# Operand starts in SBUF moved by 64 bytes: activations and split weights of a kernel's last block

## The reference, cut to what matters

```python
# 256 tokens, d = 1024, float32; two layers and then one more block
def first_block(x, ...):
    for layer in range(2):
        h = h + 0.5 * swiglu(rms_norm(h, g), w_gate, w_up, w_down)      # d_ff = 2816
        ...                                                # a convolution or attention, memory attention, w_o
        h = h + 0.5 * swiglu(rms_norm(h, g), w_gate, w_up, w_down)
def second_block(x, ...):                                  # "the last block"
    p = rms_norm(x, norm_pre) @ w_in                       # q, k, v of two mixers, gates
    ya = norm(diff_attention(...)) * silu(...)
    yb = norm(sigmoid(...) * mlstm(...)) * silu(...)
    merged = sigmoid(ga) * (ya @ w_a) + sigmoid(gb) * (yb @ w_b)
    return x + rms_norm(merged @ w_out, norm_post)
```

## The kernel before

| operand | place | modulo 256 |
| --- | --- | --- |
| whi, wlo, every slot | 0 | 128 |
| xh, xl (view of x0 and x1) | 64 | 192 |
| rh, rl | 0 | 128 |
| g in feed-forward 1, 2, 4 | 64 | 192 |
| g in feed-forward 3 | 0 | 0 |

## Time and profile before

### The profile page before, as it was taken

The page is one execution under the profiler, slowest core; times in us unless marked ns, Lnnn a source line. Parts: engine busy times, 40 slices in busy tenths (PEclk is TensorE's granted clock), DMA queues, the critical chain, the costliest instruction groups (busy, mean ns, idle before and its releaser), DMA issues.

```text
span 1186.7 us, 18987 instructions
## 1 busy us (share of the span) xinstructions
PE 1179.2 (99%) x7592; PEld 1043.9 (88%) x7592; DVE 862.0 (73%) x1213; ACT 677.7 (57%) x1036; POOL 65.5 (6%) x86
## 2 busy tenths in 40 slices
PE   9999999999999999999999999999999999999998
PEld 8888889969988888888888888998888899879996
DVE  7977766886887767787766677677776668666875
ACT  6766644547665555655554457566554545566463
POOL 1501000200010000000000022000000000000000
PEclk9999999999999999999999999999999999999999
DMA  8865656664656656656655553256655665536450
GB/s 305 305 195 180 194 176 204 210 174 137 202 189 187 190 173 195 202 172 212 192 173 173 190 177 125 74 194 193 192 184 178 194 215 173 185 125 184 144 171 35
DMA packets 65398, 215.85 MB, mean 182 GB/s; under 512 B 8352, under 2 KB 12064, under 8 KB 65184
## 3 DMA queue, kind: packets, MB, share of 16 engines
q1 hardware_dynamic: 62608, 210.64, 55.5%
q10 hardware_dynamic: 2704, 4.02, 1.0%
HBM read 212.70 MB, written 1.93 MB: 181 GB/s over the span
## 4 chain that ended last, share of the span: by engine, by line
PE 97%; DVE 1%; DMA 1%; ACT 0%; issue 0%; SPq 0%; POOL 0%; DVEq 0%; POOLq 0%
PE psum L509 96%; DMA raw<-in_slots 1%; PE psum L920 0%; DVE small L2308 0%; PE psum L1062 0%; ACT whi L1253 0%; PE psum L880 0%; PE psum L970 0%; PE psum L1011 0%; PE psum L1203 0%; PE psum L673 0%; DVE qkc L2678 0%; DVE wlo L1864 0%; PE psum L956 0%; ACT vn L1637 0%
## 5 line engine op out<-in xcount | busy, mean ns | idle before, releaser
L509 PE MATMUL psum<-x,whi 128*128 128x512 f32 (+1 forms) x2512 | 633.2, 343 | 0.2 <-DVE x L1935 0.2
L1864 DVE TENSOR_TENSOR wlo<-raw,whi 128x1024 fp32r<-128x1024 f32 (+2 forms) x402 | 474.2, 1191 | 162.1 <-ACT whi L1253 159.1
L1253 ACT CAST whi<-raw 128x1024 fp32r<-128x1024 f32 (+2 forms) x402 | 405.4, 1022 | 156.0 <-PE psum L509 151.2
L509 PE MATMUL psum<-x,wlo 128*128 128x256 f32 x1960 | 430.7, 279 | 0.0
L509 PEld LDWEIGHTS psum<-x,wlo 128*128 128x128 f32 x1960 | 366.7, 188 | 58.2 <-DVE wlo L1980 0.4
L509 PEld LDWEIGHTS psum<-x,whi 128*128 128x128 f32 x2512 | 382.1, 188 | 2.3 <-issue 1.2
L509 PE MATMUL psum<-g,whi 128*128 128x512 f32 x704 | 218.7, 392 | 0.0
L509 PEld LDWEIGHTS psum<-g,wlo 128*128 128x128 f32 x704 | 132.2, 188 | 29.5
L509 PE MATMUL psum<-whi,x 128*128 128x512 f32 (+1 forms) x512 | 140.6, 375 | 0.0
L509 PE MATMUL psum<-g,wlo 128*128 128x256 f32 x704 | 139.2, 279 | 0.0
L509 PEld LDWEIGHTS psum<-g,whi 128*128 128x128 f32 x704 | 106.8, 188 | 0.0
(11 more groups left out here) (317 smaller groups left out, 775.6 us busy)
## 6 DMA issues: line engine op xcount, KB each, us to landing
raw<-in_slots SPq DMA_DIRECT2D x371, 512.0 KB, 4.2
raw<-in_slots SPq DMA_DIRECT2D x16, 384.0 KB, 3.3
raw<-in_slots SPq DMA_DIRECT2D x16, 256.0 KB, 2.9
h<-conv_mem SPq DMA_DIRECT2D x8, 284.0 KB, 5.0
mkv<-in_mem ACTq DMA_DIRECT2D x1, 1024.0 KB, 12.4
memt<-in_mem_cols ACTq DMA_DIRECT2D x1, 1024.0 KB, 15.7
conv_mem<-hc SPq DMA_DIRECT2D x3, 288.0 KB, 2.2
h<-conv_mem SPq DMA_DIRECT2D x4, 142.0 KB, 2.9
```

Source lines behind the costliest of these rows:

```text
L509: return pe.matmul(o, l, r, start=start, stop=stop, skip_group_check=True)
L1253: act.copy(held(B.whi[:, i % SPLIT, :], *n), held(B.raw[:, i % RAW, :], *n)).then_inc(*s.hi.now(i))
L1864: dve.tensor_tensor(held(B.wlo[:, i % SPLIT, :], *n), held(B.raw[:, i % RAW, :], *n), held(B.whi[:, i % SPLIT, :], *n).bitcast(F32), ALU.s ...
```

## The change

The last block's normed activations (generation "w2") are written to and read from `rh[0]`/`rl[0]`, place 0, instead of `xh[0]`/`xl[0]`, place 64. In TensorE's code this is index 2 of a list that now has `rh[0]` behind `xh`. The split weights of 33 narrow slots (QK2, GATE2, AQK2, GAB2) stand 16 elements (64 bytes) further on in their buffers; those of the row form (VB2, VA2, ZO2) stay at the start. Each of the five buffers of `whi` and `wlo` is 32 elements (128 bytes) longer for that. To make room, `ln1` and `diag`, constants and scratch of the first layer's convolution, move into that layer's own space, and `ctap` into half of an attention buffer of the last block.

```diff
+PLACE = 32
+MOVED = {QK2 + i for i in range(9)} | {AQK2 + i for i in range(8)} | {GAB2 + i for i in range(16)}
...
+def place(i):
+    return 16 if i in MOVED else 0
+def split_slot(buffer, i):
+    return buffer[:, i % SPLIT, place(i):place(i) + SLOT]
...
-    B.whi = sb("whi", [128, SPLIT, SLOT], F32R)
-    B.wlo = sb("wlo", [128, SPLIT, SLOT], F32R)
+    B.whi = sb("whi", [128, SPLIT, SLOT + PLACE], F32R)
+    B.wlo = sb("wlo", [128, SPLIT, SLOT + PLACE], F32R)
...
-    B.diag = sb("diag", [128, 2, 128])
...
-    B.ln1 = sb("ln1", [128, 128])
...
+    B.ln1 = sb("ln1", [128, 128], F32, mx)
+    B.diag = sb("diag", [128, 2, 128], F32, mx)
...
-    T.ctap = sb("ctap", [128, 8, 4], F32, mx)
...
+    T.ctap = T.ptbuf[:, 1, 0:32].rearrange("p (k t) -> p k t", t=4)
...
-    bank, psum, xh, xl, rh, rl, ident, ones = B.bank, B.psum, B.xh, B.xl, B.rh, B.rl, B.ident, B.ones
+    bank, psum, rh, rl, ident, ones = B.bank, B.psum, B.rh, B.rl, B.ident, B.ones
+    xh, xl = B.xh + B.rh[0:1], B.xl + B.rl[0:1]
...
-        h = B.whi[:, i % SPLIT, 0:nk * n].rearrange("p (k n) -> p k n", k=nk)
-        l = B.wlo[:, i % SPLIT, 0:nk * n].rearrange("p (k n) -> p k n", k=nk)
+        h = split_slot(B.whi, i)[:, 0:nk * n].rearrange("p (k n) -> p k n", k=nk)
+        l = split_slot(B.wlo, i)[:, 0:nk * n].rearrange("p (k n) -> p k n", k=nk)
...
-            yield from rows_steps((xh[0], xl[0]), None, 8, ZO2 + 4 * i, 512, [[6], [7]], first=i,
+            yield from rows_steps((xh[2], xl[2]), None, 8, ZO2 + 4 * i, 512, [[6], [7]], first=i,
...
-        X0 = (xh[0], xl[0])
+        X0 = (xh[2], xl[2])
...
-                pair(0, 0, QK2 + 2 * c + e, c - 2, range(4 * e, 4 * e + 4), e == 0, e == 1)
+                pair(2, 0, QK2 + 2 * c + e, c - 2, range(4 * e, 4 * e + 4), e == 0, e == 1)
...
-            act.copy(held(B.whi[:, i % SPLIT, :], *n), held(B.raw[:, i % RAW, :], *n)).then_inc(*s.hi.now(i))
+            act.copy(held(split_slot(B.whi, i), *n), held(B.raw[:, i % RAW, :], *n)).then_inc(*s.hi.now(i))
...
-    ffn(3, [("w2", 7, xh[0])])
+    ffn(3, [("w2", 7, rh[0])])
...
-        pool.memset(B.ln1[:], 1.0 / 768).then_inc(*s.consts.now("ln1"))
...
     pool.wait_ge(*s.used.at(AIN - 1))
+    pool.memset(B.ln1[:], 1.0 / 768)
     pool.memset(MA.hc[:, :, 0:30], 0.0)
```

More of the change, by code:

```diff
@@ L373, in signals @@
     s.w4_first = sig("conv_weights_first", CONV_PE[:1])
-    s.consts = sig("consts", ["ones", "ident", "ln1", "upper", "identb", "mask", "half", "alib", "ident4"])
+    s.consts = sig("consts", ["ones", "ident", "upper", "identb", "mask", "half", "alib", "ident4"])
     s.fills = sig("fills", ["hc", "freq", "qk"])
@@ L1021, in gate_cols @@
         for k in range(8):
-            t = direct(bank[5][:, 0:S], h[:, k, :], l[:, k, :], 0, k, k == 0, k == 7, i if k == 0 else None)
+            t = direct(bank[5][:, 0:S], h[:, k, :], l[:, k, :], 2, k, k == 0, k == 7, i if k == 0 else None)
         t.then_inc(*s.used.now(i))
@@ L1051, in rest @@
             for k in range(8):
-                t = direct(bank[6 + c % 2][:, 0:S], h[:, k, :], l[:, k, :], 0, k, k == 0, k == 7, i if k == 0 else None)
+                t = direct(bank[6 + c % 2][:, 0:S], h[:, k, :], l[:, k, :], 2, k, k == 0, k == 7, i if k == 0 else None)
             t.then_inc(*s.used.now(i))
@@ L1105, in second @@
     def second():
-        X0 = (xh[0], xl[0])
+        X0 = (xh[2], xl[2])
         pe.wait_ge(*s.sum.at(("up", 3, PAIRS - 1)))
[L1108 to L1111, removed]
+        pair(2, 0, QK2, 2, range(4), True, False, "w2")
+        pair(2, 0, QK2 + 1, 3, range(4), True, False)
+        pair(2, 0, QK2 + 2, 2, range(4, 8), False, True, "w2")
+        pair(2, 0, QK2 + 3, 3, range(4, 8), False, True)
         pe.wait_ge(*s.h.at((6, 2)))
@@ L1120, in second @@
             for e in range(2):
-                pair(0, 0, AQK2 + 2 * c + e, (6, 7, 2, 3)[c], range(4 * e, 4 * e + 4), e == 0, e == 1)
+                pair(2, 0, AQK2 + 2 * c + e, (6, 7, 2, 3)[c], range(4 * e, 4 * e + 4), e == 0, e == 1)
                 if c == 0 and e == 0:
@@ L1863, in split_to @@
             dve.wait_ge(*s.hi.at(i))
-            dve.tensor_tensor(held(B.wlo[:, i % SPLIT, :], *n), held(B.raw[:, i % RAW, :], *n),
-                              held(B.whi[:, i % SPLIT, :], *n).bitcast(F32), ALU.subtract).then_inc(*s.lo.now(i))
+            dve.tensor_tensor(held(split_slot(B.wlo, i), *n), held(B.raw[:, i % RAW, :], *n),
+                              held(split_slot(B.whi, i), *n).bitcast(F32), ALU.subtract).then_inc(*s.lo.now(i))
             splits[0] += 1
@@ L2687, in vector_engine @@
     mix_b()
-    ffn(3, 5, [("w2", 7, (xh[0], xl[0]))])
+    ffn(3, 5, [("w2", 7, (rh[0], rl[0]))])
     second()
```

## The result

| | runs | median | ratio to before |
| --- | --- | --- | --- |
| before, in the same series | 5 | 1187.87 us (1187.33 to 1189.18) | |
| changed | 5 | 1194.93 us (1194.63 to 1195.06) | 1.0057 [1.0046, 1.0068] |

A forecast was written before the change was run, and what follows sets the result against it. PE was taken to bound the kernel, through the distance between matmul starts. Savings of 1.5 + 1.8 + 0.9 = 4.2 us from 1188.6 gave 1184.4 us (chance 0.55); range 1181.5 to 1190 us.

The forecast's parts named there:

- the slots' new stride: Split-weight buffers, whole kernel: some stand 128 bytes off modulo 256, place modulo 128 unchanged; taken to cost 0 us.
- a rival with 0.11: All feed-forward groups of four matmuls pay strongly for the 128-byte step: 8.9 us more, 1193.3 us; chance 0.11.
- The column form: Last block's 256-column matmuls, fixed operand at 64, streamed at 0: go from 117.7 to 113.3 ns; GAB2 0.9 us.
- The gain of the narrow slots: QK2, GATE2, AQK2 in the last block: 408 matmuls save 4.4 ns each at the new places, 1.8 us.
- The row form: VB2, VA2, ZO2 in the last block: 240 matmuls save 6.2 ns each with both operands at place 0, 1.5 us.
- GAB2's absorbed part: Last block: some 60 matmuls' saving becomes 0.3 us more wait of PE for `ob` at 1110 us.
- The moved memset: On POOL before `hc` is cleared: its 0.20 us is hidden by 18 us of slack, so 0.
- `ctap`: Moved into a last-block attention buffer: its last reader begins well before that half is written; no wait added, 0.
- the writes of ACT and DVE: Splits written 64 bytes on: both engines at most 76% busy, so some per cent more would be hidden; 0.
- The rival without any effect of places: Whole kernel: places don't matter as such, distances come from what surrounds a stretch; 1188.6 us; chance 0.05.

The follow-up runs named there:

- e2: Kernel before with only the 128-byte longer buffers and moved tiles; no slot placed, last block's activations left at place 64: 1195.12 us, ratio 1.0055.
- e3: Kernel before with both split-weight tiles 128 bytes further on, buffers as long as before, memory keys sharing one tile: 1189.68 us, ratio 1.0011.
- e5: As e2, but `wlo` 128 bytes further on, so `wh` and `wl` of each slot are alike modulo 256; memory keys share one tile: 1188.05 us, ratio 0.9993.
- e8: Changed kernel with `wlo` 128 bytes further on, so `wh` and `wl` are alike modulo 256 in every slot: 1187.24 us, ratio 0.9991 to the kernel before.
- e1: Changed kernel with each split-weight buffer 256 bytes longer instead of 128, memory keys sharing one tile: 1186.49 us, ratio 0.9982 to the kernel before.
- e9: On top of e1, `wh` and `wl` 128 bytes apart modulo 256 only where all matmuls have 256 columns: 1183.34 us, ratio 0.9961 to the kernel before.
- e6: As e1, but no slot placed 64 bytes on, so the column form has both operands at place 0: 1189.75 us, ratio 1.0007 to the kernel before.
- e4: Kernel before with the `wlo` tile alone 128 bytes further on, buffers as long as before, memory keys sharing one tile: 1197.30 us, ratio 1.0076.

## Why the prediction was wrong

**The step that failed** is the one on the slots' new stride: "Place (modulo 128) is unchanged ... I take 0". The step alone, e2, costs 6.3 us (1195.12 against 1188.81): some 11.4 us lost where 512 columns are streamed, by the sum above, and the rest gained in narrow slots. I had seen that the step was untested and carried it as a rival with 0.11; its middle, 1193.3 us, is 1.6 from the measured 1194.93, and its sketch (each group has one of `wh` and `wl` off, one late start delays the next) points the right way. e3 shows what being off against the streamed operand costs by itself (0.8 ns a feed-forward matmul), and e2 against e5, and e8 against the changed kernel, show that being off against each other costs much more. That the rival's middle came so near is in part luck: it starts from 1184.4, which e1 misses by 2.1 us, and knows nothing of the narrow slots' gain. What I took as evidence for 0 was none: that the row form keeps 227 ns whatever k and half it is at moves operands by multiples of 512 bytes, and the comparison of `g` and `x` by 256. (The piece at 358.02 us is the second part's `x`, not the third's; its place is 64 all the same.) Every row before had `wh` and `wl` alike modulo 256, so no row could speak, and the likeliest value had no right to be 0 at 0.8 of the chance. The range's upper end, 1190, cut off just this case.

**The column form** was the second error. I read `query_rows` as a combination of places that leaves the slow spacing by itself. e1 has that combination in column form and stays slow for 14 us until an interruption. My showed a change of form at that moment, which is an interruption too. What was measured for the 408 matmuls in e1 is a part slow, part fast, 1.2 us less in all; for GAB2 about nothing, where I had 0.9. I had reckoned with the fast spacing for all.

**The gain of the narrow slots in the changed kernel** came, 408 x 4.2 = 1.7 us against 1.8 forecast, but for another reason: e2 has it without the places, e8 has the places and less of it (WA2 and WB2 at 8.06 / 70 = 115.1 ns), and e9 shows it in slots that the change doesn't touch once `wh` and `wl` are apart and change sides from slot to slot. A number that matched the forecast stood for another mechanism.

**The row form**: 240 x 6.2 = 1.5 us forecast. In e1 the stretch gains 1.0 us. In the changed kernel its piece is at 231.4 ns, and the whole stretch is no faster than in e2, which has the old places (231.1 ns a matmul in the mean in both): there the new places gave nothing. Both operands at place 0 take 227 ns only while they are alike modulo 256 too, which e3's `merged` shows (232.4), and with the step nearly half of the row form's matmuls have them 128 bytes apart. The mechanism held, under a condition that I hadn't seen.

**GAB2's absorbed part** was forecast as a wait longer by 0.3 us. PE's wait for `ob` is 0.21 us, as before:

```profile
1117.36 0.49 PE L523 MATMUL psum<-vb,pt 128*128 128x128 f32 x2 [0.21 <-DVE ob L2639]
```

**The moved memset, `ctap`, and the writes of ACT and DVE** cost nothing, as said: ACT and DVE are as busy as before, and e5, which has the moved tiles, is level with the kernel before.

**The rival without any effect of places**: the runs are against it. e2 and e5 differ by where one tile begins, and by 7.1 us. The Trainium skill's rule (SBUF — State Buffer, "Who interferes with whom") is that TensorE's two read ports, for the streamed operand and for the weight load, are independent and that it waits on nobody. The traces disagree with the independence: the distance depends on where one operand stands to the other, 232.4 ns against 227.0 in `merged` (e3), 120.0 against 113.3 in the narrow slots (e6).

**Writes at the same time** are no explanation. ACT and DVE take as long for a split in every run (1020 to 1023 and 1191 to 1193 ns in the mean), and between 370 and 485 us the 27 groups of four matmuls during which neither of them writes one last 702.7 ns in the changed kernel and 688.6 before: the cost is there without a write.

**What stays open** is why. The runs show that the cost comes and goes with one tile of the two moved by 128 bytes. They don't show what in the memory or in TensorE does it, nor what part the alternation from slot to slot has: without it, in e4, a part of the 512-column stages escapes the cost, and the narrow slots as a whole gain little. In e4, apart but without alternation, two pieces of AQK2 give 2.73 / 23 = 118.7 and 2.75 / 24 = 114.6 ns, where the changed kernel has 113.5:

```profile
982.90 2.73 PE psum L511 x23
...
985.85 2.75 PE psum L511 x24
```

No run has `wh` and `wl` apart in the narrow slots alone without the alternation, so being apart and changing sides aren't separated.

## What to carry to other kernels

When a kernel is bound by back-to-back matmuls, starts of tiles are part of the program: compare distances between matmul starts before and after any change of a buffer's length, in the stages that the change doesn't name. Before trusting a rule such as "modulo 128", check that the trace holds a case which separates it from modulo 256; if there is none, move one tile in one run and both in another, and look at more than one stage of each: e3 is level only as a sum of gains and losses, and e4 pays in one feed-forward part and not in another. And a stretch that has one of two spacings throughout says nothing on what leads to either; look at what stood before it.

## What the runs showed of the hardware

- The distance of 512-column matmuls in row form: 226.5 to 227.1 ns in the pieces with both operands alike modulo 256; 233.2 with the fixed one 64 bytes on; 232.4 with the streamed one 128 bytes off modulo 256 (e3); 231.1 to 231.5 in the changed kernel, where nearly half are so.
- 256-column matmuls in column form: 113.3 ns or 117.7 with the operands 64 bytes apart modulo 128, either way round; 120.0 with both at place 0 (e6).
- Moving one tile by 128 bytes (e2 to e5) changed the time by 7.1 us of 1195, and moving both by the same 128 bytes (e3) by 0.9 us.
- Groups of two 512- and two 256-column matmuls with `wh` and `wl` 128 bytes apart throughout (e4): 175.7 ns a matmul or 173.4, with two small transposes at the border.
